# The last 32 tokens' experts by gathered rows on VectorE, the dense expert stages on 224 tokens, and the value product turned round

## The chip, the cores and the metric

One core of a Trainium2 chip runs the whole kernel as one program. Its engines are TensorE (PE in the profile, its weight loads PEld), VectorE (DVE), ScalarE (ACT), GpSimd (POOL) and SyncE (SP, which issues transfers); each takes its instructions in its own order, and they wait for each other by semaphores. The metric is the time of one execution on the device in microseconds, the median of several.

## The reference

A block of a hybrid model on 256 tokens of width 1024, all in float32: a mixer (attention and an RWKV-7 scan), which this change leaves alone, and then a PEER feed-forward layer with 16,384 experts, of which every token takes 8 x 16 = 128:

```python
q = (xt @ peer_wq).reshape(n_tok, PEER_HEADS, 2, PEER_HALF)
s = jnp.einsum('thpc,hpnc->thpn', q, peer_subkeys).astype(f32)
top_s, top_i = lax.top_k(s, PEER_TOPK)
cand_s = (top_s[:, :, 0, :, None] + top_s[:, :, 1, None, :]).reshape(n_tok, PEER_HEADS, kk2)
cand_i = (top_i[:, :, 0, :, None] * PEER_NKEYS + top_i[:, :, 1, None, :]).reshape(n_tok, PEER_HEADS, kk2)
best_s, best_pos = lax.top_k(cand_s, PEER_TOPK)
idx = jnp.take_along_axis(cand_i, best_pos, axis=-1)
gates = jax.nn.softmax(best_s, axis=-1)
...
u_g = peer_u[ic]
h = jax.nn.gelu(jnp.einsum('chkd,cd->chk', u_g, xc).astype(f32), approximate=False) * gc
v_g = peer_v[ic]
return jnp.einsum('chk,chkd->cd', h.astype(peer_v.dtype), v_g)
```

The result is `rmsnorm(h + peer_ffn(xn))`.

## The kernel before

The kernel is written engine by engine. The order of work is the order of the code of each engine, with loops of the device (`Fori`) of four units; nothing is scheduled by a program, except that `ranked` on VectorE deals the halves of expert units (`expert_halves`) among the ranking's instructions, one for each 2200 columns of ranking (`RANK_PER_UNIT`).

The weights come in units of 128 x 1024 numbers (512 KB). SyncE loads a unit into one of four places of `raw` as soon as the unit four before it has been multiplied. A float32 product is made of rounded parts (fp32r): ScalarE rounds a unit (`hi`, `make_hi`), GpSimd or VectorE subtracts (`lo`, `make_lo`), and the other operand is kept as `xh` (rounded) and `xl` (the rest), side by side in `xb`.

The experts' layer is computed densely, for all 16,384 experts and all tokens:

- **U stage**, 128 expert units of 128 experts each (`expert_unit`). TensorE multiplies `hi` with 512 columns (256 tokens, `xh` and `xl`) in 8 products, then `lo` with the 256 columns of `xh` in 8 more. ScalarE copies the right half out (`right_copy`), VectorE adds the halves (`expert_halves`), ScalarE applies the Gelu, and the result stands in `coef`, an expert on each partition and key and 256 columns for the tokens. GpSimd makes all `lo` of this stage.
- While the first 52 units run, VectorE ranks the scores of both tiles of 128 tokens (`top16`) and makes the picks: two key numbers and a gate for each token and pick. TensorE turns them after unit 4 x (`PICKS_AT` + 1).
- The second 64 units are **gated units** (`gated_unit`): with each, the dense gates of four tokens are made by eight one-hot products of 128 columns. VectorE makes the one-hot rows (`one_hots`), multiplies the gates into `coef` for all experts (`gates_in`) and the units' results into it (`gated`); ScalarE scales the low one-hots. `HALF` = 64 says where they begin, 4 tokens each.
- **Value stage**, 128 units of V. TensorE takes 128 tokens of `coef` (rounded `gh` and low `gl`) as weights and the unit's 512 columns as moving operand: 3 products for each of 4 banks (L910 to L912), 12 to a unit. The banks hold the result with tokens on partitions, and begin from 16 transposes of the residual `xT` (L903). ScalarE makes `gh` and `hi`, VectorE `gl` (L1968) and `lo` (L1417); GpSimd has nothing to do.
- At the end, the squares of each bank go to ScalarE, VectorE makes the inverse roots, and the four halves are scaled and stored.

In the profile L439 is the wide product and L443 the low one of a U unit; L865 and L866 are the one-hot products; L957 is ScalarE's rounding, L1358 GpSimd's split, L1917 `gates_in`, L1285 the copy of the right half.

## Time and profile before

| | |
|---|---|
| time, median of 3 runs (lowest, highest) | 1049.22 us (1048.21, 1049.79) |
| span of the profiled execution, from first to last instruction | 1046.5 us |
| TensorE busy | 1037.5 us (99%) |
| VectorE, ScalarE, GpSimd busy | 708.5, 639.7, 475.8 us (68%, 61%, 45%) |
| moved by DMA | 180.98 MB, mean 173 GB/s |

The profiled execution is known by its span; what lies around the span is in the runs' times and not in the profile, and the span is 2.7 us below the runs' median. TensorE's products are pipelined, so the time that one takes in a row (389 ns for 512 columns) is longer than the distance from its start to the next one's (227 ns); rates are read from starts.

### The profile page before, as it was taken

Reading aid. Unit: us, or ns where it says so; the run is one execution under the profiler, and the core shown is the slowest. Engines: PE = TensorE matmul, PEld = TensorE weight load, DVE = VectorE, ACT = ScalarE, POOL = GpSimd, SP = SyncE. Lnnn points to the kernel's source line nnn. Section 1 sums busy time; section 2 is a strip of 40 time slices with the busy share of each in tenths; the row PEclk is TensorE's granted clock in tenths of the full one; section 3 lists DMA queues with packets and bytes.
Section 4 is the critical chain, followed back from the end, with each engine's and each line's share of the span. In section 5 each row is a group of like instructions: output and inputs, shape, how many; then the busy total and the mean of one; then the engine's idle time right before and its main releaser. Section 6 shows DMA issues by size and latency. Waiting matters only on the chain.

```text
span 1046.5 us, 21868 instructions
## 1 busy us (share of the span) xinstructions
PE 1037.5 (99%) x6864; PEld 908.6 (87%) x6864; DVE 708.5 (68%) x1634; ACT 639.7 (61%) x1259; POOL 475.8 (45%) x228
## 2 busy tenths in 40 slices
PE   9999999999999999999999999999999999999997
PEld 8998899998898888888888888888888888888886
DVE  7765645446669999696888888865555555555554
ACT  7773575555565555657888888865454454454544
POOL 4685543883369888887777777730000000000000
PEclk9999999999999999999999999999999999999999
DMA  7463312555545555454444444455555555555553
GB/s 262 160 214 111 122 44 83 184 183 217 190 135 192 187 183 195 170 185 170 160 160 155 152 156 159 160 182 187 194 197 188 197 192 189 200 188 194 195 188 139
DMA packets 52134, 180.98 MB, mean 173 GB/s; under 512 B 5811, under 2 KB 7859, under 8 KB 51964
## 3 DMA queue, kind: packets, MB, share of 16 engines
q1 hardware_dynamic: 51660, 179.87, 50.4%
q8 instruction: 26, 0.43, 0.2%
q10 hardware_dynamic: 432, 0.55, 0.2%
q14 instruction: 16, 0.13, 0.0%
HBM read 179.34 MB, written 1.06 MB: 172 GB/s over the span
## 4 chain that ended last, share of the span: by engine, by line
PE 86%; DVE 12%; ACT 1%; DMA 0%; issue 0%; ACTq 0%; POOL 0%; DVEq 0%
PE PS L439 17%; PE PS L910 11%; PE PS L911 11%; PE PS L912 11%; PE PS L443 8%; PE PS L429 4%; PE PS L430 4%; PE PS L431 4%; PE PS L807 3%; PE PS L865 2%; PE PS L815 1%; DVE PS L1463 1%; DVE arena L1824 1%; PE PS L866 1%; DVE arena L1816 1%; DVE arena L1812 1%
## 5 line engine op out<-in xcount | busy, mean ns | idle before, releaser
L1358 POOL TENSOR_TENSOR lo<-raw,hi 128x1024 fp32r<-128x1024 f32 x191 | 463.0, 2430 | 190.2 <-ACT hi L957 178.3
L957 ACT CAST hi<-raw 128x1024 fp32r<-128x1024 f32 x331 | 346.7, 1048 | 189.3 <-DMA raw<-in_v_units 170.5
L439 PE MATMUL PS<-xb,hi 128*128 128x512 f32 x1088 | 279.3, 398 | 1.0 <-ACT arena L1243 1.0
L1417 DVE TENSOR_TENSOR lo<-raw,hi 128x1024 fp32r<-128x1024 f32 x140 | 171.7, 1226 | 148.7 <-ACT hi L957 148.7
L439 PEld LDWEIGHTS PS<-xb,hi 128*128 128x128 f32 x1088 | 194.9, 189 | 38.1 <-issue 2.4
L910 PE MATMUL PS<-hi,xb 128*128 128x512 f32 x512 | 199.4, 389 | 0.0
L912 PE MATMUL PS<-lo,xb 128*128 128x512 f32 x512 | 199.2, 389 | 0.0
L911 PE MATMUL PS<-hi,xb 128*128 128x512 f32 x512 | 199.2, 389 | 0.0
L443 PEld LDWEIGHTS PS<-xb,lo 128*128 128x128 f32 x1088 | 148.4, 190 | 11.0
L443 PE MATMUL PS<-xb,lo 128*128 128x256 f32 x1088 | 151.4, 282 | 0.0
L910 PEld LDWEIGHTS PS<-hi,xb 128*128 128x128 f32 x512 | 96.1, 188 | 20.5 <-issue 0.4
L912 PEld LDWEIGHTS PS<-lo,xb 128*128 128x128 f32 x512 | 96.1, 188 | 19.9
L911 PEld LDWEIGHTS PS<-hi,xb 128*128 128x128 f32 x512 | 96.1, 188 | 19.8
L1278 ACT ACTIVATE oh_low<-oh_high,gt 128x128 f16<-128x128 f16 x256 | 80.8, 388 | 0.0
L429 PE MATMUL PS<-xb,hi 128*128 128x256 f32 x264 | 76.0, 288 | 0.0
L430 PE MATMUL PS<-xb,hi 128*128 128x256 f32 x264 | 74.7, 283 | 0.0
L431 PE MATMUL PS<-xb,lo 128*128 128x256 f32 x264 | 74.6, 283 | 0.0
L1917 DVE SCALAR_TENSOR_TENSOR arena<-PS,arena 128x512 f32 (+1 forms) x64 | 44.2, 691 | 44.4 <-PE PS L866 44.4
L1905 DVE TENSOR_SCALAR oh_high<-PS,i2T,gT 128x128 f16<-128x128 f16 x256 | 69.9, 335 | 0.1
L1239 ACT COPY arena<-PS 128x256 f32 (+1 forms) x64 | 23.9, 373 | 60.1 <-PE PS L443 60.1
L1968 DVE TENSOR_TENSOR xb<-arena,xb 128x256 fp32r<-128x256 f32 x128 | 53.5, 418 | 1.1 <-ACT xb L1314 1.1
L1314 ACT CAST xb<-arena 128x256 fp32r (+1 forms) x128 | 51.1, 400 | 1.8 <-DVE arena L1932 1.2
(315 smaller groups left out, 1375.1 us busy)
## 6 DMA issues: line engine op xcount, KB each, us to landing
raw<-in_u_units SPq DMA_DIRECT2D x128, 512.0 KB, 3.2
raw<-in_v_units SPq DMA_DIRECT2D x128, 512.0 KB, 3.2
raw<-in_w_in_units SPq DMA_DIRECT2D x43, 512.0 KB, 3.3
raw<-in_w_q_units SPq DMA_DIRECT2D x16, 512.0 KB, 3.2
raw<-in_w_proj_units SPq DMA_DIRECT2D x8, 512.0 KB, 3.2
raw<-in_w_out_units SPq DMA_DIRECT2D x8, 512.0 KB, 3.2
arena<-bias_rows SPq DMA_DIRECT2D x2, 512.0 KB, 4.8
arena<-in_subkeys_t SPq DMA_DIRECT2D x1, 1024.0 KB, 5.4
```

The costliest lines, as they stand in the source:

```text
L429: mm(ps, hi[:, s, c], mh[:, k, :], start=(k == k0), stop=False)
L430: mm(ps, hi[:, s, c], ml[:, k, :], start=False, stop=False)
L431: last = mm(ps, lo[:, s, c], mh[:, k, :], start=False, stop=(k == k1 - 1))
L439: mm(PS[:, bank, :], hi[:, s, P * k:P * k + P], both[:, k].rearrange("p s t -> p (s t)"), start=(k == 0), stop=False, skip_group_check=True)
L443: last = mm(PS[:, bank, 0:T], lo[:, s, P * k:P * k + P], both[:, k, 0, :], start=False, stop=(k == KT - 1), skip_group_check=True)
L910: mm(o, gh[:, j, t], hi[:, w, c], start=False, stop=False, skip_group_check=True)
L911: mm(o, gl[:, j, t], hi[:, w, c], start=False, stop=False, skip_group_check=True)
L912: return mm(o, gh[:, j, t], lo[:, w, c], start=False, stop=last, skip_group_check=True)
L957: nc.scalar.copy(hi[:, j, :], raw[:, j, :]).then_inc(hi_made, 1)
L1278: last = nc.scalar.activation(oh1_low[:, j % 2, k, :], oh1[:, j % 2, k, :], ACT.Copy, scale=gt[:, bass.ds(16 * i + (4 * j + k), 1)])
L1358: nc.gpsimd.tensor_tensor(lo[:, w, :], raw[:, w, :], hi[:, w, :].bitcast(F32), ALU.subtract).then_inc(lo_pool, 1)
L1417: V.tensor_tensor(lo[:, w, :], raw[:, w, :], hi[:, w, :].bitcast(F32), ALU.subtract).then_inc(lo_dve, 1)
```

## The change

The last 32 tokens (`TG`) leave the dense stages, which keep 224 (`TD`). The dense expert products become 448 and 224 columns wide, 56 gated units make 224 tokens' gates, and 72 units are plain (`FIRST`, `SECOND`). `PICKS_AT` goes from 12 to 14, and `RANK_PER_UNIT` from 2200 to 1880, so that 56 units' halves are dealt among the ranking.

The 32 tokens' experts are taken from rows. Their inputs are turned (16 small products, `gathered_rows`), and repeated four times over the partitions (`xrep`); VectorE stages the row numbers and gates of their picks, SyncE spreads them: each partition has one token and a quarter of its 128 picks, 32. GpSimd fetches 128 rows of U by an indirect transfer, 32 times, into four places behind `coef`, and VectorE makes the dot of each row with its token (`dot`). After the 32nd, ScalarE applies one Gelu, and 32 fetches of rows of V follow, each multiplied and added to `row_sums` (`row_added`). A dot or a row sum stands behind every second unit of the value stage on VectorE.

The value product is turned round: the unit is the weight and `gh`, `gl` move, so each of 8 banks holds 128 of the 1024 outputs with the tokens in columns; a unit is 8 products of 448 columns and 8 of 224. The row sums of the four partitions of a token are added by a small product with `taker`. The residual is then added on VectorE, and 16 transposes at the end turn the result for the norm.

```diff
-HALF = NKEYS // 2
-PICKS_AT = 12
+TG = 32
+TD = T - TG
+FIRST, SECOND = 72, TD // 4
+REPS = P // TG
+GATHERS = P // REPS
+PICKS_AT = 14
...
-            with sp.Fori(0, 32) as i:
+            with sp.Fori(0, 20) as i:
+                for j in range(RAW):
+                    sp.wait_ge(unit_done, 4 * i + (U_U + j - 3))
+                    load(u_t[4 * i + j], (U_U + j) % 4)
+            sp.wait_ge(xrep_sb, 2)
+            for q in range(1, REPS):
+                sp.dma_start(xrep[TG * q:TG * q + TG, :], xrep[0:TG, :]).then_inc(xrep_in, 16)
+            sp.wait_ge(staged_made, 2)
+            sp.wait_ge(picks_ps, 3)
+            for q in range(REPS):
+                sp.dma_start(picks[TG * q:TG * q + TG], staged[P - TG:P, :, GATHERS * q:GATHERS * q + GATHERS]
+                             ).then_inc(picks_in, 16)
+            with sp.Fori(20, 32) as i:
...
+                    mm(o[:, 0:2 * TD].rearrange("p (s t) -> p s t", s=2), hi[:, w, P * k:P * k + P], xb[:, k, :, 0:TD],
+                       start=(k == 0), stop=False, skip_group_check=True)
+                pe.wait_ge(lo_pool, 4 * i + (LO_POOL_IN + j + 1))
+                for k in range(KT):
+                    last = mm(o[:, 0:TD], lo[:, w, P * k:P * k + P], xb[:, k, 0, 0:TD], start=False, stop=(k == KT - 1),
+                              skip_group_check=True)
...
+            def wide_value(j, c, start=False):
+                return mm(PS[:, V_BANKS[c], 0:2 * TD].rearrange("p (s t) -> p s t", s=2),
+                          hi[:, (U_V + j) % 4, P * c:P * c + P], xb[:, j, :, 0:TD], start=start, stop=False,
+                          skip_group_check=True)
+
+            def low_value(j, c, last=False):
+                return mm(PS[:, V_BANKS[c], 0:TD], lo[:, (U_V + j) % 4, P * c:P * c + P], xb[:, j, 0, 0:TD],
+                          start=False, stop=last, skip_group_check=True)
...
+                mm(PS[:, V_BANKS[c], 2 * TD:2 * TD + TG], row_sums[:, P * c:P * c + P], taker, start=False, stop=True,
+                   skip_group_check=True).then_inc(acc_done, 1)
+                if c >= 3:
+                    turned_out(c - 3)
...
+            act.wait_ge(rows_used, GATHERS)
+            nc.scalar.activation(pick_dot, pick_dot, ACT.Gelu).then_inc(dots_gelu, 1)
...
+            def gather(g):
+
+                rows, n = (u_rows if g < GATHERS else v_t.rearrange("n p d -> (n p) d")), g % GATHERS
+                nc.gpsimd.indirect_dma_start(
+                    out=rows_at[g % 4], out_offset=None, in_=rows,
+                    in_offset=bass.IndirectOffsetOnAxis(ap=pick_row[:, n:n + 1], axis=0)).then_inc(rows_in[g % 4], 16)
+
+            with pool.Fori(0, NKEYS // 4 - 1) as i:
                 for j in range(4):
                     make_lo(U_U, i, j)
+            pool.wait_ge(picks_in, 16 * REPS)
+            for j in range(4):
+                make_lo(U_U, NKEYS // 4 - 1, j)
+                gather(j)
             make_lo(U_V, 0, 0)
             make_lo(U_V, 0, 1)
+            for g in range(4, 2 * GATHERS):
+                pool.wait_ge(rows_used, g - 3)
+                gather(g)
...
+            def dot(b, s):
+
+                dve.wait_ge(rows_in[s], 16 * b + 16)
+                V.scalar_tensor_tensor(out=rows_at[s], in0=rows_at[s], scalar=1.0, in1=xrep[:], op0=ALU.mult, op1=ALU.mult,
+                                       accum_out=pick_dot[:, bass.ds(4 * b + s, 1)]).then_inc(rows_used, 1)
+
+            def row_added(b, s):
+
+                dve.wait_ge(rows_in[s], 16 * b + 16)
+                dve.wait_ge(rows_used, 4 * b + s)
+                V.scalar_tensor_tensor(out=row_sums, in0=rows_at[s], scalar=pick_coef[:, bass.ds(4 * b + (s - GATHERS), 1)],
+                                       in1=row_sums, op0=ALU.mult, op1=ALU.add).then_inc(rows_used, 1)
...
+            for c in range(KT):
+                dve.wait_ge(acc_done, c + 1)
+                both = PS[:, V_BANKS[c], :]
+                V.tensor_tensor(xT[:, c, :], both[:, TD:TD + T], xT[:, c, :], ALU.add).then_inc(tail_half, 1)
+                dve.wait_ge(tail_half, c + 1)
+                V.tensor_tensor(xT[:, c, 0:TD], both[:, 0:TD], xT[:, c, 0:TD], ALU.add).then_inc(tail_made, 1)
...
-RANK_FIXED, RANK_PER_UNIT = 105, 2200
+RANK_FIXED, RANK_PER_UNIT = 105, 1880
```

What stands on VectorE in the loop of the value stage: of before (`xb` is `gl`, one of four units of the loop and the beginning of the next),

```order
L1968 TENSOR_TENSOR xb<-arena,xb 128x256
L1416 REGISTER_ALU
L1417 TENSOR_TENSOR lo<-raw,hi 128x1024
L1967 REGISTER_ALU
L1968 ISA
```

and now, two units of the loop of dots with the dot behind the second (`xrep` holds the tokens, `con` takes the dot):

```order
L2077 TENSOR_TENSOR xb<-arena,xb 128x224
L1516 REGISTER_ALU
L1517 TENSOR_TENSOR lo<-raw,hi 128x1024
L2076 REGISTER_ALU
L2077 ISA
L2077 TENSOR_TENSOR xb<-arena,xb 128x224
L1516 REGISTER_ALU
L1517 TENSOR_TENSOR lo<-raw,hi 128x1024
L2082 ISA
L2083 ISA
L2083 SCALAR_TENSOR_TENSOR arena,con<-arena,xrep 128x1024
```

The low parts are 224 columns, the splits as before, and each second unit has an instruction of 1024 columns behind it.

TensorE at the program's end, of before (the last two units, one bank's six products; the same twice more behind them):

```order
L910 MATMUL PS<-hi,xb 128x512
L911 MATMUL PS<-hi,xb 128x512
L912 MATMUL PS<-lo,xb 128x512
L910 MATMUL PS<-hi,xb 128x512
L911 MATMUL PS<-hi,xb 128x512
L912 MATMUL PS<-lo,xb 128x512
```

and now (L954 wide and L959 low value products, L1019 the row sums, L1004 the transposes of the result):

```order
L954 MATMUL PS<-xb,hi 128x448 x2
L959 MATMUL PS<-xb,lo 128x224 x2
L1019 MATMUL PS<-con,hot 128x32
L1004 MATMUL PS<-con,xT 128x128 x2
L954 MATMUL PS<-xb,hi 128x448 x2
L959 MATMUL PS<-xb,lo 128x224 x2
L1019 MATMUL PS<-con,hot 128x32
L1004 MATMUL PS<-con,xT 128x128 x8
```

The transposes stood ahead of the first value unit and now stand among and behind the last one's products, with eight small products that were not there.

GpSimd at the end of the U stage, where two splits of value units were the last:

```order
L1444 TENSOR_TENSOR lo<-raw,hi 128x1024
L1484 DMA arena<-in_u_rows,con 128x1024
L1444 TENSOR_TENSOR lo<-raw,hi 128x1024
L1484 DMA arena<-in_u_rows,con 128x1024
L1444 TENSOR_TENSOR lo<-raw,hi 128x1024 x2
L1484 DMA arena<-in_u_rows,con 128x1024 x28
L1484 DMA arena<-in_v_units,con 128x1024 x32
```

Four gathers stand between the last four splits of U and the two of V, and sixty behind them.

## Rows read from the trace of the kernel before

**Rows 1.** The page: busy time of each engine; the chain that ended last.

```profile
PE 1037.5 (99%) x6864; PEld 908.6 (87%) x6864; DVE 708.5 (68%) x1634; ACT 639.7 (61%) x1259; POOL 475.8 (45%) x228
...
PE 86%; DVE 12%; ACT 1%; DMA 0%; issue 0%; ACTq 0%; POOL 0%; DVEq 0%
```

**Rows 2.** Timeline, TensorE, plain units: start us, us, engine, line, operation, count.

```profile
295.57 2.09 PE L439 MATMUL PS<-xb,hi 128*128 128x512 f32 x8
...
474.17 2.00 PE L439 MATMUL PS<-xb,hi 128*128 128x512 f32 x8
476.01 1.11 PE L443 MATMUL PS<-xb,lo 128*128 128x256 f32 x8
476.96 2.00 PE L439 MATMUL PS<-xb,hi 128*128 128x512 f32 x8
```

**Rows 3.** Timeline, a gated unit; in brackets the idle time ahead and its releaser.

```profile
519.95 0.37 ACT L1285 COPY con<-PS 128x256 f32<-128x256 f32 x1 [0.56 <-PE PS L443]
...
520.20 2.09 PE L439 MATMUL PS<-xb,hi 128*128 128x512 f32 x8
...
520.63 0.69 DVE L1917 SCALAR_TENSOR_TENSOR arena<-PS,arena 128x512 f32 x1 [0.73 <-PE PS L866]
...
522.13 1.11 PE L443 MATMUL PS<-xb,lo 128*128 128x256 f32 x8
...
522.80 2.40 POOL L1358 TENSOR_TENSOR lo<-raw,hi 128x1024 fp32r<-128x1024 f32 x1 [0.92 <-ACT hi L957]
...
523.09 0.25 PE L865 MATMUL PS<-oh_high,oh 128*128 128x128 f16 x1
```

**Rows 4.** Timeline, the beginning of the value stage, and one later unit's first product.

```profile
690.23 2.04 PE L903 MATMUL PS<-con,xT 128*128 128x128 f32 x16
...
691.70 0.75 DVE L1968 TENSOR_TENSOR xb<-arena,xb 128x256 fp32r<-128x256 f32 x2
...
692.26 0.47 PE L910 MATMUL PS<-hi,xb 128*128 128x512 f32 x1
...
850.15 0.39 PE L910 MATMUL PS<-hi,xb 128*128 128x512 f32 x1
```

**Rows 5.** Timeline, the last product and the last store's issue.

```profile
1040.45 0.39 PE L912 MATMUL PS<-lo,xb 128*128 128x512 f32 x1
...
1043.27 0.37 ACTq L1350 DMA_DIRECT2D out<-arena  x1
```

**Rows 6.** Timeline, GpSimd, plain units with no wait between.

```profile
298.98 9.49 POOL L1358 TENSOR_TENSOR lo<-raw,hi 128x1024 fp32r<-128x1024 f32 x4 [8.88 <-ACT hi L957]
```

**Rows 7.** Timeline, value stage and 50 us; page, v loads (us to landing).

```profile
853.67 1.05 ACT L957 CAST hi<-raw 128x1024 fp32r<-128x1024 f32 x1 [1.34 <-DMA raw<-in_v_units]
...
854.75 1.23 DVE L1417 TENSOR_TENSOR lo<-raw,hi 128x1024 fp32r<-128x1024 f32 x1 [1.14 <-ACT hi L957]
...
855.90 0.42 DVE L1968 TENSOR_TENSOR xb<-arena,xb 128x256 fp32r<-128x256 f32 x1
...
50.21 2.42 DVE L1573 SCALAR_TENSOR_TENSOR arena<-arena 128x1024 f32<-128x1024 f32 x1
49.14 2.41 POOL L1358 TENSOR_TENSOR lo<-raw,hi 128x1024 fp32r<-128x1024 f32 x1 [0.35 <-ACT hi L957]
...
raw<-in_v_units SPq DMA_DIRECT2D x128, 512.0 KB, 3.2
```

**Rows 8.** Warm-up's weight loads (ns min/median/max, first, last start); one behind.

```profile
L471 PEld LDWEIGHTS PS<-warm x16: 288/333/338, 1.3 to 4.5; 128*128 128x128 f32 x16
...
7.06 0.19 PEld L475 LDWEIGHTS PS<-arena,i1T 128*128 128x128 f32 x1
```

**Rows 9.** Windows, the ranking: busy time by engine, clock, DMA share, GB/s.

```profile
296.00:411.00 115.00, 115.00 (x660) 101.17 (x659) 112.30 (x447) 67.67 (x122) 100.35 (x41) 1.00 0.54 183
```

**Rows 10.** Windows, as rows 9, of the first loads and of the value stage.

```profile
4.00:9.00 5.00, 4.93 (x19) 3.79 (x18) 3.89 (x8) 4.05 (x9) 0.00 (x0) 1.00 1.03 398
...
700.00:1000.00 300.00, 300.00 (x1326) 248.48 (x1325) 172.43 (x221) 148.98 (x220) 0.00 (x0) 1.00 0.57 193
```

More of the change, by code:

```diff
@@ L936, in _ @@
+            value_lows(0, lo_pool, LO_POOL_V + 1)
+            value_ready(0, 1)
+            for c in range(KT):
+                wide_value(1, c)
+            value_lows(1, lo_pool, LO_POOL_V + 2)
             whole_unit(0, 2)
@@ L1951, in _ @@
                 one_hots(0, j + 2)
[L1952 removed]
+            with dve.Fori(1, SECOND // 4 - 1) as i:
                 for j in range(4):
@@ new lines, in _ @@
+            dot(0, 0)
+            value_operands(1, 0)
+            dot(0, 1)
+            value_operands(1, 1)
+            dot(0, 2)
+            value_operands(1, 2)
+            value_operands(1, 3)
+            dot(0, 3)
+            with dve.Fori(1, GATHERS // 4) as b:
+                for j in range(8):
+                    value_operands(2 * b + j // 4, j % 4)
+                    if j % 2:
+                        dot(b, j // 2)
+            first = GATHERS // 4
+            for j in range(4):
+                value_operands(2 * first, j)
@@ new lines, in _ @@
+            dve.wait_ge(dots_gelu, 1)
+            link(V.tensor_tensor(pick_coef, pick_dot, pick_gate, ALU.mult))
+            dve.wait_ge(rows_in[0], 16 * first + 16)
+            V.tensor_scalar(row_sums, rows_at[0], pick_coef[:, 0:1], None, ALU.mult).then_inc(rows_used, 1)
+            for j in range(4):
+                value_operands(2 * first + 1, j)
+                if j:
+                    row_added(first, j)
+            with dve.Fori(first + 1, 2 * first - 1) as b:
+                for j in range(8):
+                    value_operands(2 * b + j // 4, j % 4)
+                    if j % 2:
+                        row_added(b, j // 2)
```

295 lines of the change are left out of this document (174 added, 121 removed).

## The prediction

> **What bounds the kernel now.** I read the page's top first: TensorE is busy 99% of the span, and the chain that ended last is 86% TensorE [rows 1]. So the question for each stage is what TensorE issues there, and whether a helper would be late if it issued less. The timeline of TensorE answers the first. A plain expert unit (8 wide products of 512 columns, 8 low products of 256) takes 2.79 us (474.17 to 476.96): 1.84 wide and 0.95 low, so 119 ns for a 256-column product [rows 2]. The 64 plain units stand between 295.57 and 476.96, which is 178.7 us of such units and 2.7 of waits [rows 2]. The 64 gated units go on to 690.23, 3.33 us each: 1.93 wide, 0.96 low, and 0.44 left for eight one-hot products of 128 columns, 55 ns each [rows 2 to 4]. Behind 2.03 us of residual transposes, the 1536 products of 512 columns of the value stage begin from 692.26 to 1040.45: 227 ns apart, 2.72 us a unit, 348.6 in all with the last one's end at 1040.84 [rows 4, 5]. From that end it is 2.4 us to the last store's issue at 1043.27, and 3.2 to the end of the span [rows 5].
>
> The helpers: in a gated unit VectorE waits 0.7 us of 3.33 for TensorE, ScalarE 0.56, GpSimd 0.92 [rows 3]. In a plain unit GpSimd's split is the tightest: four back to back take 9.49 us, 2.37 each, of 2.79 [rows 6]. In a value unit VectorE waits 1.1 us for the rounding on ScalarE, and that waits 1.3 us for the load [rows 7]. All have room, but not without end.
>
> **The change, part by part.**
>
> *Fewer columns.* A wide product goes from 512 to 448 columns, a low one from 256 to 224. The slope between 256 columns (119 ns) and 512 (227 ns) is 0.42 ns a column [rows 2, 5]. A wide product so loses 27 ns and becomes 200 to 204 ns. A low one would become 105.5 ns on that line. One row has this width: the 16 warm-up products of 224 columns, whose weight loads start 213 ns apart and take 333 ns each [rows 8]. A load of as many weights at 7.06 takes 0.19 us, like those of the full clock later [rows 8]. I read that as the 1.2 GHz level for the warm-up and 2.4 GHz by 7 us, so that 213 ns become 107 at full clock, though the granted clock shown for 4 to 9 us is 1.00 [rows 10]. I take 107; above, as many weights with 128 f32 columns take 117 (16 transposes in 2.04 us, less 0.28 of the pipeline) [rows 4]. A plain unit then costs 2.79-8x0.027-8x0.012 = 2.48 us, a gated one 3.02.
> The Trainium skill (TensorE: Matmul & The Clock Gate, LDWEIGHTS) gives a weight load of 128 columns as 128/1.2 = 107 ns whatever the contraction, so the low product could not fall further with fewer tokens. By it the estimate of the unit stays 2.48 us, and the 213 ns at the half clock agree.
>
> *Fewer gated units.* Each makes the gates of four tokens, so 224 tokens need 56, and 72 units are plain. Plain: 72x2.48 = 178.6 us for 178.7. Gated: 56x3.02 = 169.1 for 213.3, **-44.2**. Do the helpers keep up? Gated, of 3.02: VectorE 3.33-0.73 = 2.6, less two operands shorter by 32 columns; ScalarE 2.77; GpSimd 2.40 [rows 3]. Plain: GpSimd 2.37 of 2.48, near but under [rows 6]. The ranking on VectorE is saturated (112.3 us of 115) and feeds the halves of 48 units before the picks [rows 9]; TensorE's 2.7 us of waits lie at its end. Now it feeds 56 units, eight halves of some 0.3 us more and the rest a little shorter, about +1 us, and the picks are due after 60 units at 295.6+60x2.48 = 444.4 us, where 52 units and the waits ended at 295.6+52x2.79+2.7 = 443.4. The same balance; I keep the 2.7 us. The sixteen small products that repeat the 32 tokens: 16x0.08 (between the 55 ns of a one-hot product and 117), **+1.3**.
>
> *Value product turned round.* Twelve products of 512 columns become 8x448 and 8x224: 8x0.202+8x0.107 = 2.47 us (2.46 to 2.55 by the bounds), 128 of them 316.2 for 348.6: **-32.4**.
>
> *What VectorE gets.* In the value stage a pair of units has two low parts (0.30 us each), two splits (1.15 from start to start, 854.75 to 855.90) and one row product of 1024 columns [rows 7]. No row has that operation with its sum: the nearest below is the split's 1.15 us, above it the same instruction on two SBUF inputs with GpSimd at work, 2.42 us [rows 7]. GpSimd has no arithmetic here, so I take 1.15: 4.05 us of 4.94, room 0.9. Where the dots turn into sums, ScalarE's Gelu stands behind the rounding of unit 69, whose load goes out when unit 65 is done, and VectorE's low part of unit 68 behind the first sum: 3.2 (landing) +1.05+0.3+0.2+1.15+0.3 = 6.2 us [rows 7], and TensorE comes for it after two units, 4.9: **+1.3** once.
>
> *Transfers.* Each pair of units adds a gather of 512 KB to two loads. A load takes a share of 0.57 of 2.72 us, 1.55; three take 4.65 of 4.94, and at the 398 GB/s of 4 to 9 us only 3.95 [rows 10]. Under the unit either way. A load lands in 3.2 us; behind a gather it would take 1.55 more. The load issued as the unit of 850.15 begins is rounded from 853.67 to 854.72 and split until 855.98; its own unit would start at 850.15+3x2.47 = 857.6, its low products at 859.2 [rows 4, 7]. That leaves 2.8 us for the rounding, 1.3 with a gather ahead, and for the split, with a gather and a row product ahead, 0.5. Cost nothing; once the cover is gone, each lost us is paid in that pair.
>
> *GpSimd.* Four gathers go between the last splits of U. The split that ends at 525.20 is of the unit after next, whose low products begin at 522.13+2x3.33 = 528.8: 3.6 us of lead, 3.0 with the shorter units, and 0.6 gained a unit (3.02-2.40) [rows 3]. The cost of an indirect issue is in no row: nothing below, a split's 2.4 us above. At 1.2 nothing waits, at 2.4 TensorE waits some 2.5 us: **+1**. SP's seven small copies go out some 16 units after what they wait for, and hold back no load.
>
> *Ends.* The residual (2.03 us) leaves the beginning of the value stage, but VectorE's first low part (from 691.70, two in 0.75) holds TensorE until about 692.2 anyway: nothing [rows 4]. It returns as ten transposes among the last products (0.11 each) with eight small products of the row sums, **+1.8**. Behind the last product now stand two additions (0.42 and 0.38), two transposes, two squares, two roots and two copies of 0.69 in one queue with a store issue between, some 5.3 us to the last issue, where it was 2.4: **+2.9** [rows 5].
>
> Sum: -0.1-44.2+1.3-32.4+1.3+1.0+1.8+2.9 = -68.4 us. The profiled execution's span of 1046.5 becomes 978.1. The runs have a median of 1049.2, 2.7 more for what lies around it: **981 us**.
>
> **Rivals.**
> *Gathers block VectorE.* The row of 2.42 us began at 50.21 while GpSimd split from 49.14 to 51.55, 1.3 us of its length; the split without GpSimd takes 1.23 [rows 7]. If each gather holds up one operation by the difference, a pair needs 4.05+1.19 = 5.24 us: 0.15x128 = +19, 1000 us. If all three large operations take 2.42, a pair takes 7.9 and the time is 981+128x1.46 = 1168, slower than before. It decides from 1.96 us of blocking a gather (0.89 of room, and 68 us over 64 pairs). For it: GpSimd reads row numbers and makes descriptors all through the stage. Against: its arithmetic is over.
> The Trainium skill (SBUF — State Buffer, Who interferes with whom) lets a VectorE instruction with two SBUF inputs contend only with a GpSimd one that reads SBUF, and infers that descriptor making needs the write side. So it would choose 981; the 2.42 us fit its first half, and no row here shows the second.
> *The transfers bind.* If gathered rows cost the DMA engines half again a load's share, a pair takes 3.5x1.55 = 5.4 us: +0.24x128 = 31, 1012 us.
> *224 columns fall off the line.* If the warm-up ran at the full clock, a low product costs 213 ns: 256x8x0.106 = +217, 1198 us, slower. It decides from 140 ns. For it: the granted clock shown. Against it: the weight loads that fell from 0.33 to 0.19 us [rows 8].
>
> **Chances.** Forecast (TensorE sets every stage) 0.66, 972 to 993 by the product's bounds and the small terms; one operation blocked, or a slower row product, 0.14; transfers bind 0.10; all blocked 0.04; off the line 0.02; something cheaper than I think 0.04. The range reaches to the two milder rivals: 970 to 1008. A measurement of this kernel can tell some 0.2% from no change. Faster 0.93, same 0.01, slower 0.06.
>
> **What would show it.** Right: wide products 200 to 204 ns apart, low ones 107; plain units 2.48, gated 3.02, value 2.47 us; TensorE still 99% busy; VectorE 80 to 85% busy in the value stage; loads of v landing in 3.2 to 4.8 us. Wrong: TensorE idle before value products with VectorE's low part or split named, splits above 1.3 us, a DMA share near 1, or GpSimd issues above 2 us apiece that make the last splits of U late.

## The result, and the profile after

| | before | after |
|---|---|---|
| median of the runs (lowest, highest) | 1049.24 us (1048.21, 1049.79) | 1021.11 us (1019.24, 1021.59) |
| span of the profiled execution | 1046.5 us | 1017.4 us |
| TensorE busy | 1037.5 us (99%) | 983.6 us (97%) |

The ratio is 0.973, with a 95% interval of 0.9717 to 0.9744. The forecast was 981 (970 to 1008): the direction was right, 40 us of the gain did not come. Against the forecast span of 978.1 us, 39.3 are missing.

The page of the changed kernel (busy time by engine; the chain that ended last), to be read beside [rows 1]:

```profile
PE 983.6 (97%) x7344; PEld 923.8 (91%) x7344; DVE 760.1 (75%) x1691; ACT 626.3 (62%) x1232; POOL 579.4 (57%) x292
...
PE 82%; DMA 11%; DVE 3%; ACT 2%; issue 1%; SPq 0%; ACTq 0%; POOL 0%; DVEq 0%
```

DMA had 0% of the chain and has 11%. That is the news of this page: transfers became late. The windows say where (columns as in [rows 9]); the first answers to the ranking there, the second to the value stage of [rows 10]:

```profile
296.00:400.00 104.00, 104.00 (x671) 98.82 (x670) 99.51 (x386) 68.54 (x124) 97.73 (x40) 1.00 0.58 201
700.00:1000.00 300.00, 284.64 (x1772) 267.97 (x1770) 228.64 (x303) 145.16 (x222) 90.06 (x53) 0.99 0.82 286
```

In the stretch of the U stage TensorE is still never idle. In that of the value stage it was busy for 300 of 300 us and is now for 284.6, and the DMA share went from 0.57 to 0.82. VectorE, which my first rival was about, is busy 76%.

The rates first. TensorE's timeline in a plain unit, as in [rows 2]:

```profile
457.14 1.80 PE L891 MATMUL PS<-xb,hi 128*128 128x448 f32 x8
458.78 1.05 PE L895 MATMUL PS<-xb,lo 128*128 128x224 f32 x8
459.67 1.60 PE L891 MATMUL PS<-xb,hi 128*128 128x448 f32 x7
```

A unit takes 2.52 us: wide products 203 ns apart (forecast 200 to 204), low ones 112 to 113 (forecast 107). GpSimd's splits still keep up, as in [rows 6] at 2.40 us each:

```profile
299.19 14.41 POOL L1444 TENSOR_TENSOR lo<-raw,hi 128x1024 fp32r<-128x1024 f32 x6 [9.01 <-ACT hi L1032]
```

Now one of the places where the value stage stands still, from 699 us on. A gather of rows of U, the last rounding that is in time, and then the late one (a number in brackets is the idle time ahead, with its releaser); first SyncE's issue of the load in question, from its own timeline:

```profile
701.50 0.33 SPq L370 DMA_DIRECT2D raw<-in_v_units  x1
...
699.84 1.22 DVE L1517 TENSOR_TENSOR lo<-raw,hi 128x1024 fp32r<-128x1024 f32 x1
699.90 1.98 POOL L1484 DMA_INDIRECT arena<-in_u_rows,con  x1 [2.04 <-DVE arena L2083]
...
702.42 1.22 DVE L2083 SCALAR_TENSOR_TENSOR arena<-arena,xrep 128x1024 f32<-128x1024 f32 x1
...
703.91 0.94 POOL L1484 DMA_INDIRECT arena<-in_u_rows,con  x1 [2.04 <-DVE arena L2083]
...
706.21 1.80 PE L954 MATMUL PS<-xb,hi 128*128 128x448 f32 x8
...
708.17 1.05 ACT L1032 CAST hi<-raw 128x1024 fp32r<-128x1024 f32 x1 [2.98 <-DMA raw<-in_v_units]
...
709.45 1.87 PE L954 MATMUL PS<-xb,hi 128*128 128x448 f32 x8 [0.56 <-ACT hi L1032]
```

Read it from the bottom. The unit after the one of 706.21 was due 2.52 us later, at 708.73, and began at 709.45, because ScalarE could round its weights only from 708.17, because the load had just landed: 6.7 us after its issue at 701.50, where a load took 3.2 before [rows 7]. The dot (1.22 us, and 0.08 for its sum) and the split (1.22) are as short as I took them; VectorE waits too.

Over the whole value stage such a place comes about every seventh unit, in some stretches every sixth. Of 125 distances between unit starts, 17 are longer than 2.77 us, and what lies above 2.52 adds up to 26.9 us. The waits between 640 and 1010 us (us in total, times, longest):

```profile
ACT hi L1032 <- DMA raw<-in_v_units: 177.1, 99, 4.6
...
PEld PS L954 <- issue: 24.9, 17, 3.7
PE PS L954 <- ACT hi L1032: 13.4, 12, 1.8
```

ScalarE's longest wait for a load is 4.6 us, of a unit of 2.52. A stall is split between PE's row and the weight loads' "issue".

Two more places cost something. The beginning of the value stage, to be laid beside [rows 4]:

```profile
650.07 4.67 POOL L1444 TENSOR_TENSOR lo<-raw,hi 128x1024 fp32r<-128x1024 f32 x2
...
652.80 2.50 DVE L2077 TENSOR_TENSOR xb<-arena,xb 128x224 fp32r<-128x224 f32 x2
...
655.15 2.76 PE L954 MATMUL PS<-xb,hi 128*128 128x448 f32 x8 [3.59 <-DVE xb L2077]
```

VectorE's first two low parts take 2.50 us where they took 0.75, and the first of them alone 2.20: it ends at 655.00, just behind GpSimd's second split (654.75). TensorE waits for it for 3.59 us, and then its eight wide products take 2.76 us and not 1.80. The granted clock says why; windows around the start, and around a stall at 825 us:

```profile
655.08:658.50 3.42, 3.35 (x12) 3.12 (x13) 2.17 (x5) 2.55 (x4) 0.00 (x0) 0.61 0.42 169
...
822.00:825.70 3.70, 2.49 (x16) 2.18 (x15) 0.00 (x0) 0.64 (x1) 0.00 (x0) 1.00 0.95 339
825.80:829.20 3.40, 2.86 (x8) 2.62 (x9) 3.07 (x5) 2.30 (x5) 0.43 (x1) 0.60 0.45 163
```

After the pause of 3.6 us, and again after one of 1.85 at 826.34, TensorE runs mostly at the level of 1.2 GHz for 3.4 us (mean 0.6 of 2.4 GHz). In the kernel before TensorE was busy for all of the 300 us of [rows 10].

The tail is as forecast: from the last low product's start at 1008.90 to the end of the span 8.5 us.

### The profile page after: what moved, and what is told of

It is laid out like the page before. It is cut to its first block, busy times and chain, and to the rows that moved or that the text cites. A ratio compares the mean times of both kernels' runs of the same rounds, so it can differ in the third digit from the quotient of the medians.

```text
span 1017.4 us, 22786 instructions
## 1 busy us (share of the span) xinstructions
PE 983.6 (97%) x7344; PEld 923.8 (91%) x7344; DVE 760.1 (75%) x1691; ACT 626.3 (62%) x1232; POOL 579.4 (57%) x292
## 4 chain that ended last, share of the span: by engine, by line
PE 82%; DMA 11%; DVE 3%; ACT 2%; issue 1%; SPq 0%; ACTq 0%; POOL 0%; DVEq 0%
PE PS L891 19%; PE PS L954 14%; PE PS L895 10%; DMA raw<-in_v_units 10%; PE PS L959 7%; PE PS L462 4%; PE PS L463 4%; PE PS L464 4%; PE PS L840 3%; PE PS L472 2%; PE PS L848 1%; PE PS L917 1%; ACT hi L1032 1%; PE PS L918 1%; PE PS L626 1%
## 5 line engine op out<-in xcount | busy, mean ns | idle before, releaser
L954 PE MATMUL PS<-xb,hi 128*128 128x448 f32 x1024 | 236.6, 372 | 22.9 <-ACT hi L1032 13.4
L891 PE MATMUL PS<-xb,hi 128*128 128x448 f32 x1024 | 235.1, 371 | 0.8 <-ACT arena L1319 0.8
L954 PEld LDWEIGHTS PS<-xb,hi 128*128 128x128 f32 x1024 | 184.2, 190 | 38.3 <-issue 24.9
L891 PEld LDWEIGHTS PS<-xb,hi 128*128 128x128 f32 x1024 | 183.0, 189 | 13.5 <-issue 1.3
L959 PEld LDWEIGHTS PS<-xb,lo 128*128 128x128 f32 x1024 | 136.0, 192 | 5.3 <-DVE lo L1517 1.1
L895 PEld LDWEIGHTS PS<-xb,lo 128*128 128x128 f32 x1024 | 133.8, 191 | 4.0
L959 PE MATMUL PS<-xb,lo 128*128 128x224 f32 x1024 | 135.9, 274 | 0.8 <-DVE lo L1517 0.8
L895 PE MATMUL PS<-xb,lo 128*128 128x224 f32 x1024 | 133.8, 273 | 0.0
L1484 POOL DMA_INDIRECT arena<-in_v_units,con x32 | 55.9, 1746 | 117.1 <-DVE hot L2090 89.7
L1484 POOL DMA_INDIRECT arena<-in_u_rows,con x32 | 49.0, 1532 | 114.3 <-DVE arena L2083 113.7
L464 PE MATMUL PS<-xb,lo 128*128 128x256 f32 x264 | 74.6, 283 | 0.0
L1357 ACT ACTIVATE oh_low<-oh_high,gt 128x128 f16<-128x128 f16 x224 | 70.8, 389 | 0.0
L1315 ACT COPY arena<-PS 128x224 f32 (+1 forms) x72 | 24.9, 346 | 44.4 <-PE PS L895 44.3
L2077 DVE TENSOR_TENSOR xb<-arena,xb 128x224 fp32r<-128x224 f32 x128 | 51.3, 401 | 0.8 <-ACT xb L1393 0.8
L462 PEld LDWEIGHTS PS<-xb,hi 128*128 128x128 f32 x264 | 50.6, 192 | 0.6 <-issue 0.2
```

The source lines that it names most:

```text
L462: mm(ps, hi[:, s, c], mh[:, k, :], start=(k == k0), stop=False)
L464: last = mm(ps, lo[:, s, c], mh[:, k, :], start=False, stop=(k == k1 - 1))
L891: mm(o[:, 0:2 * TD].rearrange("p (s t) -> p s t", s=2), hi[:, w, P * k:P * k + P], xb[:, k, :, 0:TD], start=(k == 0), stop=False, skip_gro ...
L895: last = mm(o[:, 0:TD], lo[:, w, P * k:P * k + P], xb[:, k, 0, 0:TD], start=False, stop=(k == KT - 1), skip_group_check=True)
L954: return mm(PS[:, V_BANKS[c], 0:2 * TD].rearrange("p (s t) -> p s t", s=2), hi[:, (U_V + j) % 4, P * c:P * c + P], xb[:, j, :, 0:TD], star ...
L959: return mm(PS[:, V_BANKS[c], 0:TD], lo[:, (U_V + j) % 4, P * c:P * c + P], xb[:, j, 0, 0:TD], start=False, stop=last, skip_group_check=True)
```

## Experiments

Two theories stood at first. **A**: the gathers make loads of v land late; TensorE stalls when a landing takes more than some 5.9 us (from 701.50 to 707.44, which is the due time less a rounding of 1.05 us and the 0.24 from its end to TensorE's start). **B**: VectorE's added work makes its splits late. The value stage is counted from the first wide product's start to the last low product's; "stalls" are distances of unit starts above 2.77 us, with the sum of all that is above 2.52. The ratio is to the kernel before, with its interval.

| kernel | median (lowest, highest) | ratio | value stage | stalls |
|---|---|---|---|---|
| changed kernel | 1021.1 (1019.2, 1021.6) | 0.973 [0.9717, 0.9744] | 353.7 | 17, 26.9 us |
| x1_no_gathers | 999.6 (999.0, 1000.3) | 0.9532 [0.9514, 0.9549] | 328.6 | 3, 2.9 |
| x2_short_dots | 1019.3 (1011.7, 1021.4) | 0.9724 [0.9698, 0.975] | 345.7 | 17, 20.1 |
| x4_paced | 1017.2 (1011.4, 1020.0) | 0.9706 [0.9674, 0.9738] | 339.8 | 10, 13.1 |
| x3b_half_rows | 1004.2 (1000.7, 1005.7) | 0.9568 [0.9544, 0.9592] | 333.3 | 3, 6.7 |
| x5_half_gathers | 1019.2 (1018.3, 1021.6) | 0.9717 [0.97, 0.9734] | 337.1 | 7, 10.3 |
| x6_splits_first | 1019.9 (1016.8, 1021.5) | 0.9719 [0.9697, 0.9742] | 350.2 | 16, 23.5 |
| x7_joints | 1020.1 (1008.2, 1023.4) | 0.9737 [0.9721, 0.9753] | 344.0 | 14, 18.3 |
| x8_early_loads | 1004.5 (1001.7, 1008.1) | 0.9574 [0.9554, 0.9593] | 338.4 | 5, 9.8 |
| x9_all | 999.7 (994.2, 1008.4) | 0.9547 [0.9484, 0.9609] | 334.9 | 6, 8.0 |
| x10_two_places | 1027.1 (1020.9, 1031.3) | 0.9796 [0.9748, 0.9843] | 356.1 | 19, 29.4 |
| x11_all_psum | 1002.8 (997.6, 1005.4) | 0.9575 [0.9549, 0.96] | 331.7 | 3, 3.7 |
| x12_best | 997.1 (990.5, 1001.0) | 0.9498 [0.947, 0.9526] | 332.9 | 6, 7.5 |

The stage and the stalls are those of one profiled execution each. In x2, x4, x7 and x11 that is the fastest one, 5 to 12 us below the median, and in x8 the slowest, so their stalls stand for that execution and not for the median. The executions of one kernel spread by up to 1.5% here, where those of before spread by 0.4%; a median says little about an edit of 2 us, so the small edits are judged by their place in the profile.

**x1_no_gathers.** VectorE keeps its work, the transfers go.

```diff
-            for g in range(4, 2 * GATHERS):
-                pool.wait_ge(rows_used, g - 3)
-                gather(g)
...
-                dve.wait_ge(rows_in[s], 16 * b + 16)
+                dve.wait_ge(rows_in[s], 16)
```

> The 60 gathers behind the first four are not issued; dots and row sums run on the first four fetched rows, so most of the gathered rows' part is left out while VectorE keeps its work. Theory A (loads of v land late behind gathers that come in bursts, the DMA engines being full): the value stage becomes flat at 2.52 us a unit save the start and the Gelu switch, loads land in 3 to 4 us as before, and the time falls by 25 to 30 us, to 991 to 996. Theory B (VectorE's added work makes the splits late): no change, 1018 to 1022.

21.5 us faster, by the medians. In a window of 260 us TensorE is busy for all but one, with VectorE as busy as ever, and loads land in 3.3 us (first the window, then, between 660 and 990 us, the issues with their median landing in us):

```profile
700.00:960.00 260.00, 259.04 (x1641) 245.85 (x1641) 212.41 (x282) 136.29 (x206) 0.00 (x0) 1.00 0.63 206
```

```profile
raw<-in_v_units SPq DMA_DIRECT2D x124, 512.0 KB, 3.3
```

The stage is 25.1 us shorter. The time missed the expected 991 to 996; in the execution profiled the U stage was 4.4 us longer than in the changed kernel (below, x11), which would account for it. B has fallen, A stands as far as "the gathers do it".

**x2_short_dots.** The reverse: VectorE's work goes, the gathers stay (the row sums are cut to 8 columns likewise).

```diff
-                V.scalar_tensor_tensor(out=rows_at[s], in0=rows_at[s], scalar=1.0, in1=xrep[:], op0=ALU.mult, op1=ALU.mult,
+                r = rows_at[s][:, 0:8]
+                V.scalar_tensor_tensor(out=r, in0=r, scalar=1.0, in1=xrep[:, 0:8], op0=ALU.mult, op1=ALU.mult,
```

> Dots and row sums take 8 of the 1024 columns, the gathers stay whole; most of the sums is left out. Theory A (transfers): the stalls stay, though a row place comes free at once, so that gathers come a little differently: 1010 to 1025. Theory B (VectorE's load): the stalls vanish, the value stage runs at 2.52 us a unit, 991 to 996.

As A said: VectorE falls to 151.9 us of 260 and 17 stalls are there as before, though in this execution, the fastest of four, they add up to 20.1 us and not 26.9.

**x4_paced.** One gather for each pair of units.

```diff
                 pool.wait_ge(rows_used, g - 3)
+                pool.wait_ge(unit_done, U_V + 2 * g - 6)
                 gather(g)
```

> Each gather behind the first four also waits for the unit U_V + 2g - 6 of TensorE, so that one goes out for each pair of units and no burst can form; the work is the reference's. Theory A' (the mean demand of three transfers a pair fits, only the bursts do not): the stalls mostly vanish, 994 to 1005. Theory A'' (three transfers a pair are too much in the mean): stalls stay or the whole stage is stretched evenly, 1012 to 1025. Theory B: no change.

The median lies in the range of A'', that three transfers a pair are too much, and its interval overlaps that of the changed kernel; the profiled execution, the fastest of four, has fewer stalls, 10 for 17. So bursts may have a part, and don't explain the whole. This trace has, like that of x2, the landings beside the gathers, which that of the changed kernel lacks. Issues and median landing between 660 and 990 us:

```profile
raw<-in_v_units SPq DMA_DIRECT2D x124, 512.0 KB, 5.0
...
arena<-in_v_units,con POOLq DMA_INDIRECT x32, 6.2
arena<-in_u_rows,con POOLq DMA_INDIRECT x28, 6.2
```

5.0 us for 3.3. That is the median of all loads, though a gather goes out with only every second one; I had forecast 1.55 for a load behind a gather, and nothing for the other. The longest landing is 7.3 (x2: median 4.9, longest 7.7), 11 of the 124 take more than 5.9, and the stalls are made of those. Here is one: the load, and TensorE's wait for it,

```profile
731.99 0.33 SPq L370 DMA_DIRECT2D raw<-in_v_units  x1
...
739.31 1.04 ACT L1032 CAST hi<-raw 128x1024 fp32r<-128x1024 f32 x1 [4.11 <-DMA raw<-in_v_units]
...
740.59 0.65 PE L954 MATMUL PS<-xb,hi 128*128 128x448 f32 x2 [1.21 <-ACT hi L1032]
```

and the DMA queues (packets, MB, share of 16 engines) between 733.5 and 734.75, when it had been out for 1.5 to 2.8 us, then from 734.75 to 737.5, and then from 737.5 to 739.3, when the next gather is on its way (issued at 735.11):

```profile
q0 software_dynamic: 64, 0.26, 65.7%
q1 hardware_dynamic: 2, 0.00, 0.1%
...
q1 hardware_dynamic: 217, 0.84, 77.4%
q0 software_dynamic: 44, 0.13, 12.9%
...
q0 software_dynamic: 42, 0.16, 56.4%
q1 hardware_dynamic: 64, 0.20, 27.0%
```

For 1.25 us only the gather (q0) moves, at two thirds of the engines, and no weight (q1) at all; then the queue of loads runs. So here the load does not share with the gather, it starts when that gather is nearly through. That is one part of its 7.3 us. The other comes after: from 734.75 on its queue moves 0.84 MB in 2.75 us, 1.6 times a load, and yet the load lands only at 739.3, with the next gather holding over half of the engines' time. Which packets were the last, and on which engine, the trace doesn't tell. Elsewhere, as in this last window, packets of both queues run side by side. Between 660 and 990 us a row's packet takes 213 ns in the mean, some of them over 1 us, a weight's 181; the median of both is 159.

The Trainium skill (DMA: Bandwidth & Descriptors, Queues, rings and completion order) has each DMA engine take turns between its queues, and drain a whole packet, of typically some 9 to 17 descriptors, before it switches. A packet of the profile is one row of 4 KB, so the two words don't mean the same. If the 128 rows are dealt evenly, an engine has eight of them: by the page's figure, an estimate, a whole gather may pass in one turn. The first window is in line with that and doesn't show it; whether the load's packets stood in their queue by then or were made only later, the trace doesn't tell.

**x3b_half_rows.** The same issues and the same number of rows, half the bytes (GpSimd once fills the rest of the places with zeros).

```diff
+                rows = rows.rearrange("r (h d) -> (r h) d", h=2)
...
-                    out=rows_at[g % 4], out_offset=None, in_=rows,
+                    out=rows_at[g % 4][:, 0:512], out_offset=None, in_=rows,
```

> Each gather fetches 512 of a row's 1024 columns (other numbers than the layer's are summed; GpSimd writes zeros to the rest once): the same issues, descriptors and waits, half the bytes. By now the trace shows loads of v that start only when a gather's packets are through. Theory A (a load waits for the gather's packets, so its delay goes with their bytes): landings of v mostly under 5 us, few stalls, 998 to 1006. Theory C (GpSimd's issue or the number of descriptors delays the loads): landings as long as before, 1014 to 1022.

A again, at 1004.2 us: the bytes, or the time for which they hold the engines, and neither GpSimd's issue nor the number of rows.

**x5_half_gathers.** The same bytes in two gathers, one for each unit.

```diff
-                gather(g)
+                for h in range(2):
+                    pool.wait_ge(unit_done, U_V + 2 * g - 7 + h)
+                    gather(g, h)
```

> Each row is fetched by two gathers of 512 columns, one for each unit of TensorE and not faster (bytes as in the changed kernel, twice the issues and descriptors, the layer as in the reference). Theory A (a load waits behind the one gather that is in its way, so half as big a gather costs it half as much): landings under 6 us, the stalls mostly gone, 999 to 1006. Theory A'' (three transfers' bytes a pair are too much in the mean) or C (number of descriptors): 1015 to 1030.

The time, 1019.2 us, missed A's range and lies in that of its rivals. But the value stage is at 337.1 us, 16.6 less than in the changed kernel, and it is the U stage that takes 376.5 where the others have 358 to 365. Beside x4, which holds the gathers back too, the value stage is only 2.7 us shorter; so how much of the 16.6 comes from the halving, and how much from the pacing, this run doesn't settle. The end of U, where eight issues now stand between GpSimd's splits:

```profile
647.78 2.34 POOL L1446 TENSOR_TENSOR lo<-raw,hi 128x1024 fp32r<-128x1024 f32 x1 [7.34 <-DVE pick_odd L2078]
...
655.24 0.96 POOL L1486 DMA_INDIRECT arena<-in_u_rows,con  x1 [0.16 <-issue]
...
657.48 2.37 POOL L1446 TENSOR_TENSOR lo<-raw,hi 128x1024 fp32r<-128x1024 f32 x1
...
659.90 1.15 PE L897 MATMUL PS<-xb,lo 128*128 128x224 f32 x8 [1.45 <-POOL lo L1446]
```

Two things happen here. Ahead of the last four splits GpSimd waits 7.34 us for the row numbers of the second halves, which VectorE makes only then (`pick_odd`, an addition of this run alone); unit 124 is 4.3 us longer by it. Then two issues (655.24 to 657.48) and a split are 4.6 us, for a unit of 3.05, and TensorE waits for each split: 3.2 us in the next two units, and 3.9 more ahead of the value stage. An issue is cheap where GpSimd idles, and goes into TensorE's time where it splits.

**x6_splits_first** and **x7_joints.** The second has the edit of the first, 16 transposes without use ahead of the first value unit, and the loop on ScalarE that ends with the Gelu shorter by one turn:

```diff
             for j in range(4):
                 make_lo(U_U, NKEYS // 4 - 1, j)
-                gather(j)
             make_lo(U_V, 0, 0)
             make_lo(U_V, 0, 1)
+            for j in range(4):
+                gather(j)
```

```diff
+            for k in range(16):
+                nc.tensor.transpose(PS[:, 6, P * (k % 2):P * (k % 2) + P], xT[:, k // 2, P * (k % 2):P * (k % 2) + P], ident)
             value_ready(0, 0)
...
-            with act.Fori(0, DOTS_UNITS // 4 + 1) as i:
+            with act.Fori(0, DOTS_UNITS // 4) as i:
```

> The first four gathers are issued behind GpSimd's last two splits and not between the last four of U. Theory: in the changed kernel the last split (652.41 to 654.75) overlaps VectorE's first low part, which takes 2.20 us where the others take 0.38, and TensorE waits 3.6 us for it. With the splits early, that low part takes 0.38, TensorE waits some 2.0 us, and the value stage begins 1.6 to 1.8 us earlier; time 1017 to 1021. Rival: the long low part has another cause (it waits for a result, or the first of its loop is slow), and nothing changes.

> As the run before, and two more edits: 16 transposes without use on TensorE before the first value unit, and the one Gelu of the dots four units earlier in ScalarE's order. Theory: TensorE then has no pause before the value stage, the clock's 3.4 us at 1.2 GHz there vanish and the first unit takes some 2.6 us where it took 4.2; at the switch from dots to row sums the wait of 3.7 us of VectorE for the Gelu goes, with TensorE's stall and the second drop of the clock behind it, 3 to 4 us. Together 1011 to 1016. Rivals: the transposes delay the first unit by as much as they save (the value stage begins 2 us later), or ScalarE, now earlier at the Gelu, waits for the last dot and stalls the roundings by as much.

The timeline where the value stage begins, of x6 and then of x7:

```profile
657.70 1.00 DVE L2078 TENSOR_TENSOR xb<-arena,xb 128x224 fp32r<-128x224 f32 x2
...
658.51 1.87 PE L954 MATMUL PS<-xb,hi 128*128 128x448 f32 x8 [2.06 <-DVE xb L2078]
```

```profile
651.60 1.92 PE L980 MATMUL PS<-con,xT 128*128 128x128 f32 x16
...
653.85 1.87 PE L954 MATMUL PS<-xb,hi 128*128 128x448 f32 x8 [0.33 <-DVE xb L2080]
```

With the splits early, the two low parts take 1.00 us, TensorE waits for 2.06 and not 3.59, and its clock stays up: 1.87 us for eight wide products, not 2.76. x6 has no transposes, and its first unit takes the same 2.59 us as x7's. That they are not needed doesn't follow: x10 (below), with early splits and no transposes, waits hardly longer than x6 and loses the clock, with eight products in 3.29 us; the changed kernel at the switch to the row sums keeps it behind 2.16. First x10, then the changed kernel:

```profile
659.55 3.29 PE L954 MATMUL PS<-xb,hi 128*128 128x448 f32 x8 [2.18 <-DVE xb L2078]
```

```profile
847.95 1.87 PE L954 MATMUL PS<-xb,hi 128*128 128x448 f32 x8 [2.16 <-DVE xb L2077]
```

At the Gelu the units 66 to 70 have 2.4 us above 2.52 in the changed kernel, 1.3 in x6, and 0.02 in x7. Two joints are right in the profile, 3.1 us at the start and 1 to 2 at the Gelu, and the medians don't show them: x7 missed its 1011 to 1016, at 1020.1, and the stalls behind late loads vary by more.

**x8_early_loads** and its control **x10_two_places.** Raw weights and splits share four places, so a load has to wait until TensorE has used the split. With splits in places of their own it waits only for VectorE. Two of these places come from the row places, which the control takes away alone.

```diff
+        lo_v = [lo_xb[:, 0:D], lo_xb[:, D:2 * D], lo_rows[:, 0], lo_rows[:, 1]]
...
-                    sp.wait_ge(unit_done, 4 * i + (U_V + j - 3))
+                    sp.wait_ge(lo_dve, 4 * i + (split + j - 4))
                     load(v_t[4 * i + j], (U_V + j) % 4)
```

> The splits of V are written to places of their own (two in the unused half of xb, two where the third and fourth row place was), so that a load of v goes out when the split of the unit four before it is made and not when TensorE has multiplied that unit, some 1.5 units (3 to 4 us) earlier; two row places are left. Every transfer stays as it is. Theory A (a load that waits behind a gather's packets lands in up to 7.3 us, and its rounding must begin within 6.5 us of the issue): with 3 us more lead the stalls go, the value stage runs at 2.52 to 2.54 us a unit save the start and the Gelu switch, time 995 to 1002. Theory A'' (the bytes are too many in the mean): no change, 1015 to 1022.

> The control for the early loads: two row places in place of four, and nothing else. The gathers can run ahead of the dots by less, so bursts are shorter. Theory A: stalls nearly as in the changed kernel, 1010 to 1022. Rival (the bursts that four places allow are the cause): stalls mostly gone, 997 to 1005.

16.6 us faster than the changed kernel, and 22.6 faster than the control, by the medians; the time, 1004.5, is still 2.5 us above the expected range, and the control's, 1027.1, above its own. Every transfer is still there, in less time: a window of x8,

```profile
700.00:800.00 100.00, 100.00 (x635) 95.01 (x633) 80.79 (x119) 51.47 (x79) 38.32 (x20) 1.00 0.87 308
```

has TensorE busy for 100 of 100 us at a DMA share of 0.87 and 308 GB/s, more than in the changed kernel (0.82 and 286). So the rate of the DMA engines does not bind; the lead of the loads did. And the bursts of gathers that four row places allow are not the main cause, since two places make it worse. Of the 9.8 us that are left in x8, 6.8 stand at the Gelu (units 67, 71 and 72): VectorE waits first for the Gelu (4.98 us), and then for a row (3.50, until 844.75) while ScalarE waits for a load (3.17, until 844.55), so that rows and load are late together; the third is the lower clock behind that pause.

**x9_all, x11_all_psum, x12_best.** x9 is x8 with x7's edits. In x11 VectorE also takes the gates from PSUM:

```diff
-            link(V.tensor_copy(g_high[:], gT[:]))
-            link(V.tensor_tensor(gt[:], gT[:], g_high[:], ALU.subtract))
-            ratio = con[:, C_M4 + 256:C_M4 + 512]
+            link(V.tensor_scalar(g_high[:], PS[:, 6, 0:T], GATE_UNIT, None, ALU.mult))
+            link(V.scalar_tensor_tensor(out=gt[:], in0=PS[:, 6, 0:T], scalar=GATE_UNIT, in1=g_high[:], op0=ALU.mult,
+                                        op1=ALU.subtract))
+            ratio = PS[:, 6, T:2 * T]
```

and in x12 the first two gathers go out at units 96 and 104 of U, and the third dot stands one unit later.

> The run before it in this call (early loads, two row places) with the three edits at the joints: first gathers behind the last splits, 16 transposes ahead of the first value unit, Gelu four units earlier. Theory: 4 to 6 us below that run, 990 to 997. Rival: with the splits still overlapping something else, or the Gelu late, the joints give nothing: the same time as that run.

> The second run of this call, and VectorE's instructions on the gates behind the ranking take them from PSUM (bank 6), where TensorE's transposes put them, not from a copy in SBUF. The trace of the changed kernel shows the conversion of 256 gates at 2.38 us and the subtraction at 2.51 where the same take 0.41 to 0.43 when GpSimd pauses. Theory (a VectorE instruction with all operands in SBUF waits for GpSimd's split to end): each of these takes 0.3 to 0.5 us, the waits of TensorE in units 57 to 66 (2.5 us in some runs, 6 to 7 in others) shrink, and the time is 2 to 6 us below the second run. Rival (GpSimd slows VectorE wherever the operands are): no change.

> All edits that helped (early loads with two row places, the transposes ahead of the value stage, the earlier Gelu, the gates from PSUM), and the first two gathers go out at units 96 and 104 of U, where GpSimd has 0.6 us of slack a unit, so that their rows lie ready when the value stage begins and the last splits are early too; the third dot stands one unit later. The trace of the run without this has stalls in the value units 3 to 7 (0.9, 0.1, 0.3, 0.1 and 2.3 us), where VectorE waited 2.6 and 3.3 us for rows and ScalarE 6.1 us for a load. Theory: these 3.7 us go; the value stage is 2.53 us a unit throughout, 992 to 998. Rival: the stalls come from the loads of four or five units that go out together at the stage's start, and stay with ready rows: 997 to 1003.

The conversion, the subtraction, the maximum and the product with the ratio, of x6, whose U stage lost 6.5 us in the plain units from 40 on, and then of x11:

```profile
452.78 2.38 DVE L1996 CAST g_high<-gT 128x256 f16<-128x256 f32 x1
455.19 2.51 DVE L1997 TENSOR_TENSOR gt<-gT,g_high 128x256 f32<-128x256 f32 x1
457.74 2.48 DVE L1999 TENSOR_SCALAR con<-g_high 128x256 f32<-128x256 f16 x1
...
462.34 2.47 DVE L2002 TENSOR_TENSOR gt<-gt,con 128x256 f32<-128x256 f32 x1
```

```profile
453.08 0.42 DVE L2009 TENSOR_SCALAR g_high<-PS 128x256 f16<-128x256 f32 x1
453.54 0.42 DVE L2010 SCALAR_TENSOR_TENSOR gt<-PS,g_high 128x256 f32<-128x256 f32 x1
454.00 0.43 DVE L2013 TENSOR_SCALAR PS<-g_high 128x256 f32<-128x256 f16 x1
...
457.10 0.42 DVE L2016 TENSOR_TENSOR gt<-gt,PS 128x256 f32<-128x256 f32 x1
```

2.4 us is the length of a split of GpSimd, which in the U stage is nearly always at one (97.7 us of the 104 from 296 on); with an operand or the result in PSUM the same work takes 0.42. The Trainium skill (SBUF — State Buffer, Who interferes with whom) has both halves of it, that a conversion or a `tensor_scalar` between places in SBUF can take the port pair that VectorE shares with GpSimd, as one with two SBUF inputs does, and that the other engine then waits for the whole instruction; both traces agree. In the time x11 shows nothing against x9 (1002.8 and 999.7, intervals that overlap), and neither is where it was expected (990 to 997, and 2 to 6 us below that). In the executions profiled, 2.1 us were lost in units 40 to 70 of x9 and of x11 alike, and 5.1 to 8.2 in seven of the other kernels, none of which has this edit: how often the splits fall badly differs from one execution to the next, and that the edit ends it is not shown.

x12 is the best version: 997.1 us, 5% below the kernel before and by the medians 24.0 below the changed one. Of the stalls at the stage's start one of 0.3 us is left, where x11 has 3.7 us in its units 0 to 8; as far as one execution of each tells, ready rows were what was missing there. What is left now stands at the end (distances of 5.78, 3.60 and 3.09 us), where VectorE waits for rows of V with two places, and TensorE's clock is low again behind it (2.12 us for eight wide products):

```profile
969.26 1.28 DVE L2109 SCALAR_TENSOR_TENSOR hot<-arena,con,hot 128x1024 f32<-128x1024 f32 x1 [5.07 <-DMA arena<-in_v_units,con]
...
970.99 2.12 PE L964 MATMUL PS<-xb,hi 128*128 128x448 f32 x8 [3.09 <-DVE xb L2096]
```

## Why the prediction was wrong

The 39.3 us, by the prediction's terms; each is a difference of measured and forecast.

| term | us |
|---|---|
| plain units 2.52 for 2.48 (72), gated 3.045 for 3.02 (56) | 4.3 |
| gap before the value stage 3.8 for 2.0; the 1.0 set for GpSimd's issues is this, and is taken off | 0.7 |
| value units 2.52 for 2.47 (128) | 6.4 |
| first value unit at the lower clock | 1.7 |
| stalls behind late loads (1.6 of it the lower clock behind the one at 826) | 22.8 |
| switch at the Gelu 2.4 for 1.3 | 1.1 |
| last products 4.2 for 1.8 | 2.4 |

*Transfers* is the step that failed, with "Cost nothing". Its sums held: the DMA share is 0.87 where nothing stalls (x8), not above the 0.94 of three loads of 1.55 us in 4.94, and the rate does not bind TensorE. Its slack was right too: 2.8 us by the prediction, 2.6 by the measured deadline (5.9 less 3.3). What was wrong is that I held one delay, 1.55 us for the load that has a gather ahead, against that slack. The median of all loads is up by 1.7 us, close to the 1.55 by luck, since half of them were to lose nothing; and a load that meets a gather badly pays up to 4.0 us (7.3 for 3.3), and one unit in seven stalls for it. I wrote "once the cover is gone, each lost us is paid" and gave that case no time. x1 prices the whole: the stage is 25.1 us shorter without gathers, and x8 gets 15.3 of it back with the gathers in place. Of the rivals, "the transfers bind" had the right place and the nearest time, 1012 us, by the wrong mechanism: rate for lead.

*Fewer columns*: the low product is 112 to 113 ns and not 107. Between the bounds of 105.5 and 117 I took what the warm-up's 213 ns give when halved. Eight of them are 0.05 us a unit, 6.4 us over the 128 value units and most of the 4.3 in U; the wide product (203) was right.

*Fewer gated units*, *Value product turned round* and the tail behind the last product (8.5 us) were right but for that size. The switch at the Gelu was seen, at half its price; ScalarE waits 1.45 us for a load just ahead of it, so a part may be a late load.

*GpSimd* had its cost in the wrong place. The issues among them (0.94 to 1.98 us each for rows of U) delayed no split that TensorE waited for; they moved the last split into VectorE's first low part, which it blocks. *Ends* failed with it, in "nothing": I let the 16 transposes go since VectorE held TensorE for as long anyway, and did not ask what TensorE does meanwhile. Without them it pauses, and after 3.6 us of pause it also pays for the clock.

*Gathers block VectorE*: refuted. The dots take 1.22 us and the splits 1.22 with gathers issued all through. The rule for this case of the Trainium skill (SBUF — State Buffer, Who interferes with whom), which the prediction cited, held.

What the loads do behind a gather, wait in the queue or come into it late, stays open, and so does why some land late long after it. No run put an ordinary transfer of the same size in the gather's place, so that it must be gathered rows is not shown. Of the 4.2 us at the last products a part is late weights (TensorE waits 0.56 us for ScalarE at 1000.77 and 0.79 for VectorE at 1002.03); the rest was not tried by itself.

## What to carry to other kernels

Hold the worst landing against the slack of a load, not the mean one: when a stream of gathers is added, ask what a load costs that meets a whole one, and if the slack is less, give it lead before anything else. Here the lead lay in a place that was kept for its second user (the split) and not for the load. When work is taken from in front of a wait because the wait hides it, ask what it hid in turn: the clock, and the moment at which two engines' instructions on SBUF meet.

## What the runs showed of the hardware

- A gather of 128 rows of 4 KB and a load of 512 KB on the same DMA engines shared them unevenly: for 1.25 us of x4 the queue of loads moved nothing with a load out since 731.99. Landings went from 3.3 us (x1) to 5.0 in the median, 7.3 at most (x4).
- DMA sustained a share of 0.87 and 308 GB/s for 100 us beside a TensorE that never waited (x8).
- An indirect issue of 128 rows held GpSimd for 0.94 to 1.98 us for U (1.53 in the mean) and up to 3.42 for V (1.75), in the changed kernel; in x12 13 of the 32 for V took 3.42.
- A conversion of 256 columns from SBUF to SBUF took 2.38 us beside GpSimd's splits (x6), and 0.42 from PSUM (x11).
- TensorE went to the level of 1.2 GHz for some 3.4 us behind waits of 3.59 and 1.85 us (changed kernel) and 2.18 (x10), and did not behind waits of 2.16 (changed kernel) and 2.06 (x6): the length of the wait alone did not decide it.
